# A turned copy ahead of the third group's exponentials, and rotary angles made inside the last feed of the first block

## The chip, the cores and the metric

One core of one Trainium2 chip runs the whole program. The metric is the device time in microseconds. The kernel before was timed three times: 2276.24 us is the median (2274.07 to 2278.8). All times below are microseconds from the start of the span of one profiled execution.

## The reference

Two model blocks run one after the other on 256 tokens of width 1024, in float32, each with two layers.

- The first block's layer is a mixer, a layer norm, a feed and a layer norm. The mixer makes 10 projections of `x`; two attention groups A and B of 4 heads (A with rotary turns on q and k, B with a forgetting bias), a spatial gating branch and a pooling branch; the four results are joined and multiplied by `w_o`. The feed is `h = x @ w_up`, a causal convolution of width 3 along the tokens, `silu(gate) * val`, then `@ w_down` (inner width 2816).
- The second block's layer is an RMS norm, a mixer with a delta-rule branch, a sparse attention branch and a memory branch, and a gated feed.
- The second block's sparse attention turns its q, k and index vectors by angles that depend on the input `positions`:

```python
ang = positions.astype(jnp.float32)[..., None] * inv_freq
cos = jnp.cos(ang)[:, :, None, :]
```

So the tables of sines and cosines of the second block depend on `positions` alone, and not on `x`.

## The kernel before

**One stream of weights.** All large products go through one object, `Stream` (`main`). The weights are cut into chunks of 1 MB, called sources; a source is two halves of 128x1024. For each half, SyncE (SP) loads the raw weights into one of 3 slots (L328), ScalarE (ACT) makes a rounded copy `w_hi` (`high`, L339), GpSimd (POOL) makes the rest `w_lo = w_raw - w_hi` (`low`, L348), and TensorE (PE) does three products per tile (L147, L148, L149). There are 4 slots for `w_hi` and `w_lo`, so `high` of half h waits for the product of half h-4. The load of source n waits until `low` of the last half of source n-3 is done. A unit is one named piece of the stream with its output bank and with what ACT and VectorE (DVE) do at its end.

**Order by hand.** Each engine runs its own program in order. A stage calls `main.act(act, pos)`, `main.dve(dve, pos)` or `main.pe(pe, pos)`, which issues all of the stream's work up to that half, and then adds its own instructions. For ACT, position q issues `high` of half q+3 first, then what the units that end there want. For DVE there is only what units want at their ends. SP runs the `sp` functions of the stages in the order of the stages, and `send(sp, upto)` issues the loads of the stream up to a source, each after its wait.

**The first block's mixer** (`Mixer1`) has four score groups: 0 and 1 are branch A's first and second 128 queries, 2 and 3 are branch B's. A group goes through `scores` (PE), `weigh` (DVE: mask, maximum, L728 to L731), `exponentials` (ACT, L631), `normalise` (DVE: reciprocal L738, product with it L739), `turn` (PE transposes, L524), `turned_copy` (ACT copies the transposes to SBUF, L639), `weighted` (PE, L534), `weighted_high` (ACT, L649) and a low part (DVE, L819). `weigh(2)` and `weigh(3)` wait for `turn(0)` and `turn(1)`, since they write over the same score tiles. PE's `turn(1)` waits for `turned_copy(0)`, for `weigh(2)`'s mask and for `normalise(1)`. PE's `weighted(0)` waits for `weigh(3)`'s mask, and `turn(2)` behind it for `normalise(2)`. PE's `weighted(1)` waits for `turned_copy(2)`.

**The first block's feed** (`Feed1`) has 33 units of two halves each: unit 0 up0, 1 val0, 2 up1, 3 val1, 4 down0, 5 up2, 6 val2, 7 down1, 8 up3, 9 val3, 10 down2, 11 up4 and so on. At the end of an up or val unit ACT makes the first tap and DVE the other two (L876). After a val unit DVE makes `hid` (L888). After up2 DVE also makes the low part of `hid` of pair 1 (`hid_lo`, L898), which the products of down1 wait for (`hid_low`); in general the low part of pair i-1 is made at the end of up i.

**SP in the last feed of the first block.** The stage ahead of the feed is `Norm1` with the key `ln1`. Its `sp` function is `send` up to 12 sources past the last source of the mixer, that is up to unit 11 of the feed. In layer 0 a DMA of `ln_rows` follows it (L1058). `Norm1` with the key `ln2` then sends the rest of the feed.

**The start of the second block.** The last `Norm1` ends the first block, `Norm2` normalises for the second (its low parts, `x_lo`, L1146), and `Mixer2` begins. Its first unit is `sm` (two halves). Its halves 0 to 3 have their `w_hi` and `w_lo` before the norm. ACT issues `high` of halves 4 and 5, reads `small` and `ik` from the bank of `sm` (L1347, L1348), makes exponentials and logarithms in turns with DVE (L2079 to L2099), and only then issues `high` of half 6. In front of all this DVE has `angles` (L2180 to L2191) and ACT has two Sin activations (L1899, L1900), for the tables of the sparse attention. The positions are loaded by SP at the same place (L1535).

Of the kernel before, what the change touches and what calls it, by code (L numbers as in the profile page):

```python
# [23 lines left out]
I32 = mybir.dt.int32  # L24
ALU = mybir.AluOpType
ACT = mybir.ActivationFunctionType
AX_X = mybir.AxisListType.X

P = 128
T = 256  # L30
# [3 lines left out]
DEPTH = 2  # L34
# [98 lines left out]
class Chain:  # L133
# [5 lines left out]
    def step(self, ins):  # L139
        self.n += 1  # L140
        ins.then_inc(self.sem, 1)
        self.eng.wait_ge(self.sem, self.n)
# [278 lines left out]
class Mixer1:  # L421
# [199 lines left out]
    def act(self, act):  # L621
# [3 lines left out]
        def exponentials(g):  # L625
            name, qt, qk, y0, v0 = self.groups[g]
            nk = (qt + 1) * P
            act.wait_ge(*sig.at("shifted", l, g))
            for h in range(4):
                v = m["sm"][g][:, h, 0:nk]  # L630
                ins = act.activation(v, v, ACT.Exp, bias=m["mx"][:, g, h:h + 1], scale=0.125,  # L631
                                     accum_out=m["sum"][:, g, h:h + 1])
            ins.then_inc(*sig.up("exped", l, g))
# [45 lines left out]
        exponentials(1)  # L679
        main.act(act, self.at(17))  # L680
        exponentials(2)
        main.act(act, self.at(18))
        turned_copy(0)
        main.act(act, self.at(19))
# [24 lines left out]
    def dve(self, dve):  # L709
# [100 lines left out]
        weigh(2)  # L810
        normalise(1)
        weigh(3)
        normalise(2)
        normalise(3)
# [9 lines left out]
class Feed1:  # L824
# [107 lines left out]
    def pe(self, pe):  # L932
        self.net.main.pe(pe, self.end())

    def act(self, act):
        self.net.main.act(act, self.end())

    def dve(self, dve):
        self.net.main.dve(dve, self.end())

# [380 lines left out]
class Mixer2:  # L1321
# [209 lines left out]
    def sp(self, sp):  # L1531
        net, l, sig, m = self.net, self.l, self.net.sig, self.net.mem2
        if l == 0:
            sp.wait_ge(*sig.at("x_final", 3))
            sp.dma_start(m["turns"][:, 0, :].bitcast(I32), net.a["positions"].to_broadcast([P, T])  # L1535
                         ).then_inc(*sig.up("pos_loaded", by=16))
        net.main.send(sp, net.main.halves[self.u["sm"].first + 76][0])
        sp.wait_ge(*sig.at("scored2", l, 3))
        sp.dma_start(m["mem"], net.a["mem"].rearrange("(t p) d -> p t d", p=P)).then_inc(*sig.up("mem_loaded", l, by=16))
# [345 lines left out]
    def act(self, act):  # L1885
# [10 lines left out]

        if l == 0:
            act.wait_ge(*sig.at("reduced"))
            act.activation(net.tables[:, 2:4, :], m["angle"][:, :, :], ACT.Sin).then_inc(*sig.up("sined", 0))  # L1899
            act.activation(m["half_sine"][:, :, :], m["angle"][:, :, :], ACT.Sin, scale=0.5).then_inc(*sig.up("sined", 1))  # L1900
        main.act(act, self.at(2))
# [167 lines left out]
    def dve(self, dve):  # L2069
        net, l, sig = self.net, self.l, self.net.sig  # L2070
        K, main, m, bank = net.K, net.main, net.mem2, net.bank
        step, prm = net.dve_chain.step, net.prm2
        if l == 0:
            self.angles(dve)
        dve.tensor_scalar(m["half_bias"][:, :], prm(l, "b_gate"), 0.5, None, ALU.mult).then_inc(*sig.up("half_bias", l))
# [93 lines left out]
        main.dve(dve, 2 * (self.units[-1].last + 1))  # L2169

    def angles(self, dve):
        net, sig, m = self.net, self.net.sig, self.net.mem2
        K, step = net.K, net.dve_chain.step
        magic = 1.5 * 2.0 ** 23
        c1 = 6.28125
        c2 = float((np.float32(2 * np.pi - c1).view(np.int32) // 4096 * 4096).astype(np.int32).view(np.float32))
        c3 = 2 * np.pi - c1 - c2
        pos, a, k, h = m["pos"][:, :], m["angle"][:, :, :], m["turns"][:, :, :], m["half_sine"][:, :, :]
        dve.wait_ge(*sig.at("pos_loaded"))
        step(dve.tensor_copy(pos, m["turns"][:, 0, :].bitcast(I32)))  # L2180
        for j in range(2):
            ins = dve.tensor_scalar(a[:, j, :], pos, K("freq")[:, j:j + 1], None, ALU.mult)
        step(ins)
        step(dve.tensor_scalar(k, a, 1.0 / (2 * np.pi), magic, ALU.mult, ALU.add))
        step(dve.tensor_scalar(k, k, magic, None, ALU.subtract))
        for c in (c1, c2, c3):
            step(dve.scalar_tensor_tensor(a, k, -c, a, ALU.mult, ALU.add))
        dve.tensor_scalar(a, a, 3.1415925, -3.1415925, ALU.min, ALU.max).then_inc(*sig.up("reduced"))
        dve.wait_ge(*sig.at("sined", 1))
        step(dve.tensor_tensor(h, h, h, ALU.mult))  # L2190
        step(dve.tensor_scalar(net.tables[:, 0:2, :], h, -2.0, 1.0, ALU.mult, ALU.add))  # L2191

# [197 lines left out]
class Net:  # L2390
# [88 lines left out]
    def second_memory(self, area):  # L2479
# [11 lines left out]
        m["set"] = [[place(f"{n}_set{hf}", 16 * hf + 4 * i, [P, 4, T])[:, :, :] for i, n in enumerate("qkvz")] for hf in range(2)]  # L2491
        m["pos"], m["turns"] = place("pos", 16, [P, T]), place("turns", 17, [P, 2, T])
        m["angle"], m["half_sine"] = place("angle", 19, [P, 2, T]), place("half_sine", 21, [P, 2, T])
        m["half"] = h = {}
# [78 lines left out]
    def run(self):  # L2573
        nc, sig, a, main, const = self.nc, self.sig, self.a, self.main, self.const
        xT = self.xn[:, :, :].rearrange("p t (k c) -> p (t k) c", c=T)
        with nc.Block() as block:
            @block.sync
            def _(sp):
# [16 lines left out]
                for s in self.stages:  # L2595
                    if isinstance(s, (Norm1, Norm2, Mixer2, Final)):
                        s.sp(sp)
# [105 lines left out]
```

## Time and profile before

| what | us |
|---|---|
| median of 3 runs | 2276.24 |
| the profiled execution's own time | 2277.58 |
| its span | 2275.8 |
| PE busy | 2163.2 (95%) |
| POOL busy | 1498.6 (66%) |
| ACT busy | 1073.0 (47%) |
| DVE busy | 955.9 (42%) |
| mean granted TensorE clock | 0.972 of full |

PE is busy for 95% of the span, so time is won or lost where PE stands still, or where its clock is granted at half. Busy time of the other engines matters only where PE, at that moment, waits for them. The matmuls' ends in the records are modelled: a matmul with 256 columns is shown as 0.28 us and one starts every 0.12 us at full clock.

### The profile page before, as it was taken

What the parts mean: (1) busy time and instruction counts of PE and PEld (TensorE: products, weight loads), DVE (VectorE), ACT (ScalarE), POOL (GpSimd) and SP (SyncE); (2) the same over time, 40 slices, a digit from 0 to 9 for tenths busy, and PEclk for the clock granted to TensorE, in tenths of its full rate; (3) what the DMA queues carried; (4) which work ended last, traced back from release to release, by engine and by line L of the source; (5) the groups of instructions that cost most, each with busy time, mean ns of one, the idle gap of its engine ahead of it and who ended that gap; (6) DMA issues with size and microseconds to landing.
All of it is one profiled execution on the core that took longest, in us unless ns stands there. A gap on an engine that the chain in (4) does not pass through costs nothing.

```text
span 2275.8 us, 35984 instructions
## 1 busy us (share of the span) xinstructions
PE 2163.2 (95%) x15336; PEld 2001.3 (88%) x15336; DVE 955.9 (42%) x1484; ACT 1073.0 (47%) x1517; POOL 1498.6 (66%) x632
## 2 busy tenths in 40 slices
PE   8989989899969899999999899998999999999998
PEld 7789978799959888989999899898889899998998
DVE  4353256442375537477112211456374681123112
ACT  4555555555545352255444444473441454544444
POOL 6679877698846234356778688663243566786886
PEclk9999999999989999999999999999999999999999
DMA  8345544355524113134445455442131344454553
GB/s 338 132 146 204 185 139 161 117 180 187 184 84 147 60 71 106 64 128 167 151 164 185 148 185 185 156 145 90 56 112 56 130 148 149 157 182 150 184 185 133
DMA packets 47183, 333.05 MB, mean 146 GB/s; under 512 B 5168, under 2 KB 5552, under 8 KB 7856
## 3 DMA queue, kind: packets, MB, share of 16 engines
q1 hardware_dynamic: 47024, 330.76, 41.9%
q8 instruction: 121, 1.98, 0.4%
q14 instruction: 38, 0.31, 0.0%
HBM read 329.69 MB, written 1.05 MB: 145 GB/s over the span
## 4 chain that ended last, share of the span: by engine, by line
PE 62%; DVE 8%; issue 1%; ACT 1%; POOL 0%; DVEq 0%; ACTq 0%
PE bank L147 14%; PE bank L149 14%; PE bank L148 14%; PE y L147 2%; PE y L149 2%; PE y L148 2%; PE bank L1749 2%; PE bank L1748 1%; PE bank L1739 1%; DVE conv L1384 1%; PE bank L1672 1%; PE bank L1794 1%; PE bank L1791 1%; PE bank L1774 1%; DVE sq L1583 1%
## 5 line engine op out<-in xcount | busy, mean ns | idle before, releaser
L348 POOL TENSOR_TENSOR w_lo<-w_raw,w_hi 128x1024 fp32r<-128x1024 f32 x602 | 1463.0, 2437 | 759.7 <-ACT w_hi L339 759.6
L339 ACT ACTIVATE w_hi<-w_raw 128x1024 fp32r<-128x1024 f32 x602 | 635.7, 1059 | 1009.4 <-PE bank L149 838.9
L147 PE MATMUL bank<-x_hi,w_hi 128*128 128x256 f32 x2960 | 876.6, 296 | 21.6 <-POOL w_lo L348 17.1
L148 PE MATMUL bank<-x_lo,w_hi 128*128 128x256 f32 x2960 | 848.4, 287 | 0.0
L149 PE MATMUL bank<-x_hi,w_lo 128*128 128x256 f32 x2960 | 848.3, 287 | 0.0
L147 PEld LDWEIGHTS bank<-x_hi,w_hi 128*128 128x128 f32 x2960 | 579.1, 196 | 44.9 <-issue 24.4
L148 PEld LDWEIGHTS bank<-x_lo,w_hi 128*128 128x128 f32 x2960 | 579.0, 196 | 10.5 <-issue 8.6
L149 PEld LDWEIGHTS bank<-x_hi,w_lo 128*128 128x128 f32 x2960 | 578.4, 195 | 0.0
L876 DVE SCALAR_TENSOR_TENSOR conv<-bank,par_sb,conv 128x254 f32<-128x254 f32 (+1 forms) x176 | 76.8, 478 | 240.1 <-ACT conv L864 238.6
L1246 DVE TENSOR_TENSOR hid_lo<-hid,hid_hi 128x512 fp32r<-128x512 f32 x22 | 45.1, 2048 | 241.2 <-ACT hid_hi L1241 241.2
L147 PE MATMUL y<-w_hi,hid_hi 128*128 128x512 f32 x352 | 139.9, 397 | 3.3 <-DVE hid_lo L898 3.3
L149 PE MATMUL y<-w_hi,hid_lo 128*128 128x512 f32 x352 | 138.9, 395 | 0.0
L148 PE MATMUL y<-w_lo,hid_hi 128*128 128x512 f32 x352 | 138.9, 395 | 0.0
L1384 DVE SCALAR_TENSOR_TENSOR conv<-bank,par_sb,conv 128x255 f32<-128x255 f32 (+1 forms) x144 | 62.6, 477 | 63.8 <-ACT conv L1375 62.1
L147 PEld LDWEIGHTS y<-w_hi,hid_hi 128*128 128x128 f32 x352 | 66.3, 188 | 19.2 <-DVE hid_lo L898 5.4
L149 PEld LDWEIGHTS y<-w_hi,hid_lo 128*128 128x128 f32 x352 | 66.2, 188 | 15.7
L148 PEld LDWEIGHTS y<-w_lo,hid_hi 128*128 128x128 f32 x352 | 66.2, 188 | 13.8
L1491 DVE SCALAR_TENSOR_TENSOR gate<-gate,bank 128x512 f32<-128x512 f32 x16 | 11.0, 688 | 130.5 <-PE bank L149 130.5
L1749 PE MATMUL bank<-ti,es 128*128 128x128 f32 x320 | 61.0, 290 | 4.1 <-DVE es L2275 4.1
L1748 PE MATMUL bank<-es,ti 128*128 128x128 f32 x256 | 51.8, 286 | 7.0 <-DVE es L2275 7.0
L1749 PEld LDWEIGHTS bank<-ti,es 128*128 128x128 f32 x320 | 49.6, 205 | 4.5 <-DVE es L2275 4.5
L2347 DVE SCALAR_TENSOR_TENSOR sc<-index,tokq,sc 128x128 f32<-128x128 f32 (+1 forms) x28 | 52.6, 1878 | 1.0
(397 smaller groups left out, 3243.6 us busy)
## 6 DMA issues: line engine op xcount, KB each, us to landing
w_raw<-w SPq DMA_DIRECT2D x300, 1024.0 KB, 4.8
ln_rows<-ln_rows SPq DMA_DIRECT2D x4, 1024.0 KB, 7.2
mem_tok<-mem SPq DMA_DIRECT2D x2, 1024.0 KB, 4.9
const_sb<-const SPq DMA_DIRECT2D x1, 1536.0 KB, 9.3
par_sb<-par SPq DMA_DIRECT2D x2, 553.5 KB, 10.7
xn<-xT SPq DMA_DIRECT2D x1, 1024.0 KB, 4.9
w_raw<-w SPq DMA_DIRECT2D x2, 512.0 KB, 5.4
x_tok<-x SPq DMA_DIRECT2D x1, 1024.0 KB, 7.2
```

What stands on the lines that cost most here:

```text
L147: pe.matmul(out, lhs[0], rhs[0], start=start, stop=False, skip_group_check=skip)
L148: pe.matmul(out, lhs[0], rhs[1], start=False, stop=False, skip_group_check=skip)
L149: return pe.matmul(out, lhs[1], rhs[0], start=False, stop=stop, skip_group_check=skip)
L339: act.activation(self.hi[:, h % HALVES, :], self.raw[:, n % RAWS, i * HW:(i + 1) * HW], ACT.Copy).then_inc(*sig.up("high", h))
L348: pool.tensor_tensor(self.lo[:, h % HALVES, :], self.raw[:, n % RAWS, i * HW:(i + 1) * HW], self.hi[:, h % HALVES, :].bitcast(F32), ALU.su ...
L876: ins = dve.scalar_tensor_tensor(cb[:, j, tap:T], view[:, j, 0:T - tap], taps[:, 2 - tap, c0 + j:c0 + j + 1], cb[:, j, tap:T], ALU.mult, A ...
L1246: dve.tensor_tensor(net.hs2[1][:, 2 * (i % 3):2 * (i % 3) + 2, :], m["hid"][:, i % 2, :, :], net.hs2[0][:, 2 * (i % 3):2 * (i % 3) + 2, :] ...
L1384: ins = dve.scalar_tensor_tensor(cb[:, j, tap:T], two(b)[:, j, 0:T - tap], taps[:, 3 - tap, c0 + j:c0 + j + 1], cb[:, j, tap:T], ALU.mult, ...
L1583: net.dve_chain.step(dve.tensor_tensor(raw, raw, cos.unsqueeze(1).to_broadcast([P, w, T]), ALU.mult))
L1748: pe.matmul(yd[g][:, c], h["ti"][:, n, :], h["y"][:, n, :], start=True, stop=True)
L1749: mm = pe.matmul(cp[g][:, c], h["y"][:, n, :], h["ti"][:, n, :], start=True, stop=True)
L2347: ins = dve.scalar_tensor_tensor(sc, m["r"][qt][:, (h % 2) * 4 + h // 2, :], m["tokq"][:, qt, 4, h:h + 1], mask if h == 0 else sc, ALU.mul ...
```

## The change

Three edits. First, in the mixer of the first block (both layers), ACT makes `turned_copy(0)` before `exponentials(2)`, and DVE makes `normalise(2)` before `weigh(3)`. Second, the angles of the second block are made in the feed of layer 1 of the first block: DVE's operations stand in pairs behind the units 4, 7, 10, 13, 19 and 22, ACT's two Sin activations behind unit 16. Third, the load of the positions moves to a new `sp` function of `Feed1`, and `Feed1` is added to the stages whose `sp` is called; the four tiles of the angles lie at other addresses, over constants that only the first block's mixer reads.

```diff
@@ Mixer1.act
         main.act(act, self.at(17))
+        turned_copy(0)
+        main.act(act, self.at(18))
         exponentials(2)
-        main.act(act, self.at(18))
-        turned_copy(0)
         main.act(act, self.at(19))
@@ Mixer1.dve
         normalise(1)
+        normalise(2)
         weigh(3)
-        normalise(2)
         normalise(3)
@@ Feed1
+    def after_unit(self, n):
+        return 2 * (self.units[n].last + 1)
+
+    def sp(self, sp):
+        net, sig, m = self.net, self.net.sig, self.net.mem2
+        if self.l == DEPTH - 1:
+            sp.wait_ge(*sig.at("var", "ln1", self.l, 1))
+            sp.dma_start(m["turns"][:, 0, :].bitcast(I32), net.a["positions"].to_broadcast([P, T])
+                         ).then_inc(*sig.up("pos_loaded", by=16))
@@ Feed1.act
+            main.act(act, self.after_unit(16))
+            act.wait_ge(*sig.at("reduced"))
+            act.activation(net.tables[:, 2:4, :], m["angle"][:, :, :], ACT.Sin).then_inc(*sig.up("sined", 0))
+            act.activation(m["half_sine"][:, :, :], m["angle"][:, :, :], ACT.Sin, scale=0.5).then_inc(*sig.up("sined", 1))
@@ Feed1.dve
+            main.dve(dve, self.after_unit(4))
+            dve.wait_ge(*sig.at("pos_loaded"))
+            step(dve.tensor_copy(pos, m["turns"][:, 0, :].bitcast(I32)))
+            for j in range(2):
+                ins = dve.tensor_scalar(a[:, j, :], pos, net.K("freq")[:, j:j + 1], None, ALU.mult)
+            step(ins)
+            main.dve(dve, self.after_unit(7))
+            step(dve.tensor_scalar(k, a, 1.0 / (2 * np.pi), magic, ALU.mult, ALU.add))
+            step(dve.tensor_scalar(k, k, magic, None, ALU.subtract))
+            main.dve(dve, self.after_unit(10))
+            for c in (c1, c2):
+                step(dve.scalar_tensor_tensor(a, k, -c, a, ALU.mult, ALU.add))
+            main.dve(dve, self.after_unit(13))
+            step(dve.scalar_tensor_tensor(a, k, -c3, a, ALU.mult, ALU.add))
+            dve.tensor_scalar(a, a, 3.1415925, -3.1415925, ALU.min, ALU.max).then_inc(*sig.up("reduced"))
+            main.dve(dve, self.after_unit(19))
+            dve.wait_ge(*sig.at("sined", 1))
+            step(dve.tensor_tensor(h, h, h, ALU.mult))
+            main.dve(dve, self.after_unit(22))
+            step(dve.tensor_scalar(net.tables[:, 0:2, :], h, -2.0, 1.0, ALU.mult, ALU.add))
@@ Mixer2.sp, Mixer2.act, Mixer2.dve: the same operations are taken out
-        if l == 0:
-            sp.wait_ge(*sig.at("x_final", 3))
-            sp.dma_start(m["turns"][:, 0, :].bitcast(I32), ...)
...
-        if l == 0:
-            act.wait_ge(*sig.at("reduced"))
...
-        if l == 0:
-            self.angles(dve)
@@ Net.run
-                    if isinstance(s, (Norm1, Norm2, Mixer2, Final)):
+                    if isinstance(s, (Norm1, Feed1, Norm2, Mixer2, Final)):
                         s.sp(sp)
```

## Rows read from the trace of the kernel before

**Rows 1.** The page's chain that ended last: shares of the span by engine.

```profile
PE 62%; DVE 8%; issue 1%; ACT 1%; POOL 0%; DVEq 0%; ACTq 0%
```

**Rows 2.** Waits of PE: us in total, times, longest.

```profile
PE t L524 <- ACT pt L639: 4.3, 2, 2.1
```

**Rows 3.** Timeline, start of block two: start, us, engine, line, [idle before <-releaser].

```profile
652.35 1.28 ACT L1899 ACT_TABLE_LOAD   x1
653.32 0.28 DVE L2180 CAST pos<-turns 128x256 f32<-128x256 int32 x1
660.03 4.78 POOL L348 TENSOR_TENSOR w_lo<-w_raw,w_hi 128x1024 fp32r<-128x1024 f32 x2 [25.41 <-ACT w_hi L339]
660.22 2.27 DVE L2075 TENSOR_SCALAR half_bias<-par_sb 128x24 f32<-128x24 f32 x1
660.81 1.13 ACT L1347 ACTIVATE small<-bank 8x256 f32<-8x256 f32 x3
662.68 2.29 DVE L2079 TENSOR_SCALAR y<-small,par_sb 8x256 f32<-8x256 f32 x1
665.79 0.59 PE L1598 MATMUL bank<-ik,const_sb 128*128 128x256 f32 x2
670.53 1.99 ACT L339 ACTIVATE w_hi<-w_raw 128x1024 fp32r<-128x1024 f32 x2
671.65 14.30 POOL L348 TENSOR_TENSOR w_lo<-w_raw,w_hi 128x1024 fp32r<-128x1024 f32 x6 [6.83 <-ACT w_hi L339]
674.05 0.45 PE L147 MATMUL bank<-x_hi,w_hi 128*128 128x256 f32 x1 [4.79 <-POOL w_lo L348]
677.69 0.28 PE L149 MATMUL bank<-x_hi,w_lo 128*128 128x256 f32 x1
```

**Rows 4.** Windows: PE, PEld, DVE, ACT, POOL busy (x), PEclk, DMA share, GB/s.

```profile
82.50:85.00 2.50, 0.35 (x4) 0.30 (x4) 0.37 (x1) 2.50 (x7) 0.75 (x1) 1.00 0.71 295
```

**Rows 5.** Timeline of SP: weight loads and the DMA behind one.

```profile
174.61 0.33 SPq L328 DMA_DIRECT2D w_raw<-w  x1
174.98 0.43 SPq L1058 DMA_DIRECT2D ln_rows<-ln_rows  x1
...
488.90 0.33 SPq L328 DMA_DIRECT2D w_raw<-w  x1
```

**Rows 6.** DMA issues: KB each, us from issue to landing.

```profile
w_raw<-w SPq DMA_DIRECT2D x300, 1024.0 KB, 4.8
turns<-positions SPq DMA_DIRECT2D x1, 128.0 KB, 2.9
```

**Rows 7.** Timeline of the last feed of block one, units 5 to 8.

```profile
477.24 1.78 DVE L876 SCALAR_TENSOR_TENSOR conv<-bank,par_sb,conv 128x255 f32<-128x255 f32 x4 [8.58 <-ACT conv L864]
478.94 2.25 DVE L898 TENSOR_TENSOR hid_lo<-hid,hid_hi 128x512 fp32r<-128x512 f32 x1
481.24 0.50 PE L147 MATMUL y<-w_hi,hid_hi 128*128 128x512 f32 x1 [0.35 <-DVE hid_lo L898]
483.65 17.49 POOL L348 TENSOR_TENSOR w_lo<-w_raw,w_hi 128x1024 fp32r<-128x1024 f32 x7
```

**Rows 8.** Timeline of the first block's mixer, layer 0.

```profile
57.85 2.69 DVE L748 TENSOR_TENSOR aqk<-aqk,const_sb 128x512 f32<-128x512 f32 x1
79.92 0.69 DVE L728 TENSOR_TENSOR sm<-s,forget 128x512 f32<-128x512 f32 x1 [10.31 <-PE t L524]
81.65 1.23 DVE L739 TENSOR_TENSOR sm<-sm,rc 128x1024 f32<-128x1024 f32 x1
84.08 0.57 ACT L639 ACTIVATE pt<-t 128x512 f32<-128x512 f32 x1
84.70 1.09 PE L524 MATMUL t<-const_sb,sm 128*128 128x128 f32 x8 [2.15 <-ACT pt L639]
89.87 0.66 PE L524 MATMUL t<-const_sb,sm 128*128 128x128 f32 x4 [0.71 <-DVE sm L739]
93.23 1.14 PE L534 MATMUL o<-pt,abv 128*64 128x128 f32 x16
```

More of the change, by code:

```diff
@@ L933, in pe @@
         self.net.main.pe(pe, self.end())
-    def act(self, act):
-        self.net.main.act(act, self.end())
-    def dve(self, dve):
-        self.net.main.dve(dve, self.end())
+    def after_unit(self, n):
[6 more added lines that the diff above has]
+                         ).then_inc(*sig.up("pos_loaded", by=16))
@@ new lines, in act @@
+    def act(self, act):
+        net, sig, m, main = self.net, self.net.sig, self.net.mem2, self.net.main
+        if self.l == DEPTH - 1:
+            main.act(act, self.after_unit(16))
+            act.wait_ge(*sig.at("reduced"))
+            act.activation(net.tables[:, 2:4, :], m["angle"][:, :, :], ACT.Sin).then_inc(*sig.up("sined", 0))
+            act.activation(m["half_sine"][:, :, :], m["angle"][:, :, :], ACT.Sin, scale=0.5).then_inc(*sig.up("sined", 1))
+        main.act(act, self.end())
@@ new lines, in dve @@
+    def dve(self, dve):
+        net, sig, m, main = self.net, self.net.sig, self.net.mem2, self.net.main
+        if self.l == DEPTH - 1:
+            step = net.dve_chain.step
+            magic = 1.5 * 2.0 ** 23
+            c1 = 6.28125
+            c2 = float((np.float32(2 * np.pi - c1).view(np.int32) // 4096 * 4096).astype(np.int32).view(np.float32))
+            c3 = 2 * np.pi - c1 - c2
+            pos, a, k, h = m["pos"][:, :], m["angle"][:, :, :], m["turns"][:, :, :], m["half_sine"][:, :, :]
+            main.dve(dve, self.after_unit(4))
[18 more added lines that the diff above has]
+            step(dve.tensor_scalar(net.tables[:, 0:2, :], h, -2.0, 1.0, ALU.mult, ALU.add))
+        main.dve(dve, self.end())
@@ L1532, in sp @@
         net, l, sig, m = self.net, self.l, self.net.sig, self.net.mem2
-        if l == 0:
-            sp.wait_ge(*sig.at("x_final", 3))
-            sp.dma_start(m["turns"][:, 0, :].bitcast(I32), net.a["positions"].to_broadcast([P, T])
-                         ).then_inc(*sig.up("pos_loaded", by=16))
         net.main.send(sp, net.main.halves[self.u["sm"].first + 76][0])
@@ L1895, in key_log @@
                            ).then_inc(*sig.up("key_inverse", l, hf, j))
-        if l == 0:
-            act.wait_ge(*sig.at("reduced"))
-            act.activation(net.tables[:, 2:4, :], m["angle"][:, :, :], ACT.Sin).then_inc(*sig.up("sined", 0))
-            act.activation(m["half_sine"][:, :, :], m["angle"][:, :, :], ACT.Sin, scale=0.5).then_inc(*sig.up("sined", 1))
         main.act(act, self.at(2))
@@ L2169, in dve @@
         main.dve(dve, 2 * (self.units[-1].last + 1))
[L2171 to L2191, printed above, removed]
     def prepare_dve(self, dve, hf, unit_key):
@@ L2491, in second_memory @@
         m["set"] = [[place(f"{n}_set{hf}", 16 * hf + 4 * i, [P, 4, T])[:, :, :] for i, n in enumerate("qkvz")] for hf in range(2)]
-        m["pos"], m["turns"] = place("pos", 16, [P, T]), place("turns", 17, [P, 2, T])
-        m["angle"], m["half_sine"] = place("angle", 19, [P, 2, T]), place("half_sine", 21, [P, 2, T])
+        m["pos"], m["turns"] = place("pos", 0, [P, T]), place("turns", 1, [P, 2, T])
+        m["angle"], m["half_sine"] = place("angle", 3, [P, 2, T]), place("half_sine", 5, [P, 2, T])
         m["half"] = h = {}
```

## The prediction

> **What bounds the kernel now.** I read the page first, its chain of waits: 62% of the span by TensorE (PE) and 8% by VectorE (DVE) [rows 1]. PE is the bound, so I look only for places where PE stands still or runs at half clock, and ask what each part of the change does there. Then I read PE's waits and the timelines of three places. At the start of block two PE stands still for 4.79 us until the low part of half 6 is made [rows 3]. In each mixer of block one it waits 2.15 us ahead of `turn(1)` for `turned_copy(0)` (4.3 us over two layers, [rows 2]) and 0.71 us ahead of `turn(2)` for `normalise(2)` [rows 8]. In the last feed of block one it hardly waits: 0.35 us ahead of down1 [rows 7]. So the change has about 4.8 + 2 x 2.9 us of stalls to win, and the feed is where something can be lost.
>
> **Part 1, the angles leave the start of block two.** DVE's angles begin at 653.32, and `half_bias`, which follows them, at 660.22 [rows 3]. Without them `half_bias` can start at 653.4. The next step, `y`, then waits for ScalarE's (ACT) copies of `small` and `ik`. These need the product of half 1. Half 4's product ends at 665.79 [rows 3] and a half is 24 matmuls at 0.12 us = 2.88 us, so half 1 ends at 657.15. ACT makes `high` of half 5 first (1.0 us), then the copies (1.13 + 0.39), and ends at 659.9. Meanwhile GpSimd (POOL) makes the low part of half 5, from about 658.5 to 660.9. `half_bias` took 2.27 us for 24 columns: it began 0.19 us after a POOL operation and ended when that ended (660.03 + 2.39); `y`, at 662.68, ended with the second [rows 3]. So I let `y` end with POOL again, at 661.05 instead of 664.97: 3.9 us earlier. The chain behind it (exponential, logarithm, scans, to `high` of half 6 at 670.53) has nothing that moves otherwise, so half 6's low part comes at 670.15 and PE, which has ended half 5 at 669.2, stands still for 0.9 us instead of 4.79.
>
> After the stall of 4.79 us the clock was half: the 17 matmuls from 674.05 to 677.69 took 3.64 us instead of 2.04, a loss of 1.6 us [rows 3]. A stall of 2.15 us left the clock full (1.00 in that window, [rows 4]), so a stall of 0.9 us will too. Part 1 gives 3.9 + 1.6 = **-5.5 us**. Its ends are -6.4 (no stall is left) and -3.5 (0.4 us later, clock still half).
>
> **Part 2, the wait for the positions in the feed.** DVE waits for `pos_loaded` behind unit 4, in front of unit 5 (up2). SP, though, comes to `Feed1.sp` only after `Norm1.sp`, which sends the stream up to unit 11. The load of unit 11 waits for the low part of unit 8's last half. Layer 0 shows the same place in SP's order: `ln_rows` was issued at 174.98, 0.37 us behind a weight load at 174.61; in layer 1 the corresponding weight load is at 488.90 [rows 5]. POOL's run from 483.65 has two halves (2.5 us each) ahead of it, 16 and 17, the halves of unit 8 [rows 7]. So the positions are asked for at 489.3. With DVE standing still, POOL isn't held up by it (about 1 us in its last operations), so I put the issue at 488.3.
>
> Who waits? Behind the waiting DVE instruction stands all of up2's work: its taps (477.24 before) and `hid_lo` of pair 1 (478.94 before), and down1's first matmul, at 481.24, waits for that [rows 7]. There is no deadlock: the low part of half 17 needs only the product of half 13 (val2), which needs nothing of DVE behind unit 4. But PE stops in front of down1.
>
> Landing: alone the positions took 2.9 us, a weight load 4.8 [rows 6]. Bounds: 488.3 + 2.9 = 491.2; behind the whole weight load, 487.9 + 4.8 = 492.7 and some 1.7 us for its own small packets, 494.4. I take 493.5, near the upper end, since the weight load is asked for only 0.4 us ahead. Then DVE: the copy and the first two products, 1.0 us (three short operations like the 0.28 us copy); taps to `hid_lo` 478.94 - 477.24 = 1.70; `hid_lo` 0.7 instead of 2.25, as POOL is idle. PE starts down1 at 493.5 + 3.45 = 496.95, against 481.24: **+15.7 us**. Restart at half clock: +1.6, as in part 1. POOL's backlog is worked off in the stall, so the next waits for `hid_lo` (0.35 to 0.4 us each) may go: -0.4. Sum of part 2: **+16.9 us**, between +14.6 (lands at 491.2) and +19.5.
>
> The other feed pieces I cost at nothing. DVE was idle for 8.58 us ahead of up2's taps [rows 7], behind the down unit, and up3, up4 and so on have the same gap; two operations of 0.7 us, each held up by POOL by at most 2.4, need 6.2. ACT's Sin pair behind unit 16 costs two table loads (1.28 us each [rows 3]) and two activations under 1.0 us, at most 4.6 us, in a stream that is four halves (11.5 us) ahead of PE. Were that cover gone, each would cost its own length once.
>
> **Part 3, the mixer's two swaps.** ACT can start `turned_copy(0)` when DVE starts `weigh(2)` on the same release, 79.92 [rows 8]. Before, it came behind the exponentials, at 84.08. By that alone PE would start `turn(1)` when `normalise(1)` ends, 82.9 instead of 84.70: -1.8, and with the 0.71 us -2.5 a layer. But ACT now goes on to `high` of half 21 at 80.39 and POOL starts its low part 1.12 us later (670.53 to 671.65 is this distance, [rows 3]), at 81.52. `normalise(1)`'s product, two SBUF inputs, comes at 81.65 [rows 8], 0.13 us behind. A product of that kind, L748, started at 57.85 in a POOL operation and took 2.69 us instead of 0.69 [rows 8]. So here it ends at 83.91 + 1.1 = 85.0 and `turn(1)` starts at 85.05, not earlier than before. Then `normalise(2)` (85.25) falls behind the low part of half 22 (85.0 to 87.4) and ends at 87.95; `weigh(3)`, now behind it, has its mask at 89.2 and its maximum at 90.65; `exponentials(3)` ends at 92.65, `high` of half 23 and one small copy follow, and `turned_copy(2)` ends at 94.45. PE reaches `weighted(1)` at 93.23 as before [rows 8] and waits till 94.5. That is **+1.25 us a layer, +2.5 in all**. From the other side, if the product gets in first, POOL waits for it and `normalise(2)` waits for POOL: `turned_copy(2)` at 92.4, -0.85 a layer; with no collision at all -2.5 a layer. Ends: -4.9 and +3.5; I take +2.5, since 0.13 us decides and stands on POOL's side in both layers, which have equal spacings.
>
> The trace agrees with the Trainium skill's page "SBUF — State Buffer", section "Who interferes with whom": DVE with two SBUF inputs and a GpSimd operation that reads SBUF exclude one another, and the one that issues first holds the port for its whole instruction. By a rule that shared bandwidth instead, `normalise(1)` would end near 83.3 and this part would gain, not lose; 57.85 to 60.54 speaks against it.
>
> **Sum.** -5.5 + 16.9 + 2.5 = +13.9 us. On the profiled execution's own time, 2277.58 (span 2275.8), that is 2291.5; it lies 1.3 above the median of the runs, 2276.24, from which it is 2290.1. I say 2291.
>
> **The rivals.**
> - A. *The stall is there, the mixer swaps win.* For it: PE's waits of 2.15 and 0.71 us are real, and 0.13 us is a thin margin. -5.5 + 16.9 - 1.7 = +9.7, 2287; with no collision +6.5, 2284. Chance 0.2.
> - B. *The positions land before DVE asks* (this one ends on the other side). It needs SP to issue them before the low part of half 13 or so, that is, to be at `Feed1.sp` by the time unit 4 ends (about 469). Then DVE's idle 8.58 us hides the three short operations, part 2 is zero, and -5.5 +2.5 gives 2274 (-5.5 - 4.9 gives 2267). It decides at a landing by about 476, before up2's taps; each us later costs one. Against it: SP's order and the 174.98 of layer 0. Chance 0.08.
> - C. *The gain of part 1 does not come*: something else holds half 6, as ACT's chain now waits for POOL's second low part at each small DVE operation. Each adds up to 2.4 us; +13.9 + 5.5 = 2297. For it: `half_bias` and `y` were both held up. Against it: POOL is idle from 660.9 on until half 6. Chance 0.1.
>
> **How the numbers follow.** Main case 0.62, 2291 (its own range 2288 to 2295, from the bounds of the landing). A, B and C as above. The range 2283 to 2297 holds the main case, all of A and C. A measurement of this kernel can tell 0.2%, 4.6 us, from no change. Slower by more: the main case, A (its no-collision end is +6.5) and C: 0.91. Within 0.2%: part of B, 0.04. Faster: the rest of B, 0.05.
>
> **What would show it.** In the profile after: the load of positions by SP directly behind the weight load near 488; DVE idle from 468.7 until about 493; one PE stall of some 15 us ahead of down1, released by `hid_lo` (L898), the largest of the whole profile outside the norms, with half clock behind it. At the start of block two: a stall under 1.5 us with clock 1.00. In the mixer: the product of L739 in group 1 near 3.3 us long instead of 1.23, and PE waiting ahead of `weighted(1)` for ACT's `pt`. The forecast is wrong if the positions are issued much before 488, or if PE passes down1 on time.

## The result and the profile after

The changed kernel takes 2290.26 us (median of 4 runs, 2289.86 to 2292.14) against 2276.09 us for the kernel before in runs beside it: a ratio of 1.0063, interval 1.0046 to 1.0081. That is 14.2 us slower. The prediction was 2291 us. The profiled execution after took 2289.86 us with a span of 2288.1, 12.3 us more than the span before. The profiled execution before was 1.5 us above the median of its kernel and this one 0.4 us below, which is the 1.9 us between the two differences.

First the waits of PE, in us, times and longest, of the kernel after.

```profile
PE y L147 <- DVE hid_lo L898: 18.1, 7, 15.5
PE bank L147 <- POOL w_lo L348: 13.4, 3, 11.4
PE t L524 <- DVE sm L739: 5.0, 2, 2.5
...
PE o L534 <- ACT pt L639: 1.2, 1, 1.2
```

The same list of the kernel before:

```profile
PE bank L147 <- POOL w_lo L348: 17.1, 3, 11.4
...
PE y L147 <- DVE hid_lo L898: 3.3, 8, 0.5
```

The wait for `hid_lo` grew by 14.8 us, by one stall of 15.5 us. The wait for POOL's low part fell by 3.7 us. In the mixer the wait for `turned_copy` of 4.3 us [rows 2] is gone, and 5.0 us for DVE's `sm` (1.4 us before) stand in its place, with 1.2 us ahead of `weighted(1)`.

**The feed.** Timelines after: start, us, engine, line, [idle before <-releaser]. The first two rows are SP's, the next two POOL's, then DVE's, and PE's first matmul of down1.

```profile
489.80 0.33 SPq L328 DMA_DIRECT2D w_raw<-w  x1
490.18 0.43 SPq L942 DMA_DIRECT2D turns<-positions  x1
...
485.14 4.64 POOL L348 TENSOR_TENSOR w_lo<-w_raw,w_hi 128x1024 fp32r<-128x1024 f32 x2
504.25 2.39 POOL L348 TENSOR_TENSOR w_lo<-w_raw,w_hi 128x1024 fp32r<-128x1024 f32 x1 [14.47 <-ACT w_hi L339]
...
469.07 1.58 DVE L888 TENSOR_TENSOR hid<-gates,conv 128x512 f32<-128x512 f32 x1
494.92 0.29 DVE L965 CAST pos<-turns 128x256 f32<-128x256 int32 x1 [24.27 <-DMA turns<-positions]
495.25 0.62 DVE L967 TENSOR_SCALAR angle<-pos,const_sb 128x256 f32<-128x256 f32 x2
495.90 1.78 DVE L876 SCALAR_TENSOR_TENSOR conv<-bank,par_sb,conv 128x255 f32<-128x255 f32 x4
497.60 0.68 DVE L898 TENSOR_TENSOR hid_lo<-hid,hid_hi 128x512 fp32r<-128x512 f32 x1
...
498.33 0.80 PE L147 MATMUL y<-w_hi,hid_hi 128*128 128x512 f32 x1 [15.45 <-DVE hid_lo L898]
```

Read it from the bottom: PE waits 15.45 us for `hid_lo`, which is made as soon as the taps are; the taps stand behind the two products and the copy; and these wait for the positions, which SP asked for directly behind a weight load. That load was free to go when POOL ended the second of its two halves (485.14 + 4.64). DVE stood idle for 24.27 us.

Windows after, columns as in [rows 4]: behind that stall, and at the start of block two.

```profile
498.30:502.30 4.00, 3.97 (x10) 3.15 (x11) 3.09 (x7) 0.10 (x1) 0.00 (x0) 0.55 0.00 0
688.30:692.30 4.00, 3.97 (x33) 3.98 (x34) 3.89 (x10) 3.94 (x7) 4.00 (x2) 1.00 0.16 27
```

PE did 10 matmuls in 4 us at a granted clock of 0.55 (0.5 is half) after 15.45 us idle. At the start of block two the clock is full. Its timeline after:

```profile
671.43 0.17 DVE L2109 TENSOR_SCALAR half_bias<-par_sb 128x24 f32<-128x24 f32 x1
678.05 1.15 DVE L2113 TENSOR_SCALAR y<-small,par_sb 8x256 f32<-8x256 f32 x1 [6.20 <-ACT ik L1392]
688.33 0.38 PE L147 MATMUL bank<-x_hi,w_hi 128*128 128x256 f32 x1 [0.96 <-POOL w_lo L348]
```

`half_bias`, which took 2.27 us in [rows 3], takes 0.17, and the stall of 4.79 us is one of 0.96.

**Where the time went.** Both programs have the same 15336 matmuls in the same order, so the stretch between two matmuls of the same number can be subtracted. The mixer stretches hold `turn(1)` and `weighted(1)` (81.5 to 93.7 and 394.1 to 413.3 us in the profile before), the feed's is 480.3 to 500.4 and that of block two 651.5 to 680.0. In us:

```
stretch                                      before   after   difference
mixer of block one, layer 0                    12.2    13.3     +1.1
mixer of block one, layer 1                    19.2    20.1     +0.9
last feed, with down1                          20.2    36.3    +16.1
start of block two                             28.4    23.1     -5.3
the rest                                     2189.3  2188.8     -0.5
start of the span to the last matmul         2269.3  2281.6    +12.3
```

The rest hides stretches of block two that moved by -2.4 to +1.7 us each, though the change touches nothing in them.

**The mixer of layer 0**, timeline after:

```profile
80.82 2.37 POOL L348 TENSOR_TENSOR w_lo<-w_raw,w_hi 128x1024 fp32r<-128x1024 f32 x1 [1.19 <-ACT w_hi L339]
81.00 3.27 DVE L739 TENSOR_TENSOR sm<-sm,rc 128x1024 f32<-128x1024 f32 x1
84.39 2.65 DVE L739 TENSOR_TENSOR sm<-sm,rc 128x512 f32<-128x512 f32 x1
84.41 1.06 PE L524 MATMUL t<-const_sb,sm 128*128 128x128 f32 x8 [2.51 <-DVE sm L739]
```

POOL starts 0.18 us ahead of the product of `normalise(1)`, which takes 3.27 us where it took 1.23 [rows 8], and PE stands still for 2.51 us. From there the two layers differ. Windows after, layer 0 (first two) and the same place in layer 1:

```profile
84.40:86.40 2.00, 1.99 (x11) 1.77 (x12) 2.00 (x1) 0.96 (x2) 2.00 (x1) 0.77 0.00 0
86.40:88.40 2.00, 2.00 (x6) 1.57 (x5) 1.97 (x3) 0.14 (x1) 0.09 (x1) 0.50 0.45 111
...
401.00:405.00 4.00, 3.97 (x26) 3.13 (x27) 3.96 (x3) 1.02 (x1) 1.92 (x1) 1.00 0.27 61
```

and PE at `weighted(1)`, in layer 0 and in layer 1:

```profile
93.70 1.15 PE L534 MATMUL o<-pt,abv 128*64 128x128 f32 x16
...
409.92 1.15 PE L534 MATMUL o<-pt,abv 128*64 128x128 f32 x16 [1.20 <-ACT pt L639]
```

In layer 1 the clock stays full and PE waits 1.20 us for `turned_copy(2)`. In layer 0 the clock falls to half, which costs PE about as much, and it arrives late enough to find the copy ready. Why the clock fell in one layer and not in the other isn't shown.

### The profile page after: what moved, and what is told of

Read it like the earlier page. It is cut to its first block, busy times and chain, and to the rows that moved or that the text cites. A ratio compares the mean times of both kernels' runs of the same rounds, so it can differ in the third digit from the quotient of the medians.

```text
span 2288.1 us, 35988 instructions
## 1 busy us (share of the span) xinstructions
PE 2162.6 (95%) x15336; PEld 2000.1 (87%) x15336; DVE 971.5 (42%) x1484; ACT 1071.9 (47%) x1516; POOL 1503.0 (66%) x632
## 4 chain that ended last, share of the span: by engine, by line
PE 60%; DVE 9%; ACT 1%; issue 1%; POOL 0%; DVEq 0%; ACTq 0%
PE bank L147 13%; PE bank L148 13%; PE bank L149 13%; PE y L147 2%; PE y L149 2%; PE y L148 2%; PE bank L1789 2%; PE bank L1788 1%; DVE sc L2359 1%; PE bank L1779 1%; DVE conv L1428 1%; PE bank L1712 1%; PE bank L1831 1%; PE bank L1834 1%; PE bank L1814 1%
## 5 line engine op out<-in xcount | busy, mean ns | idle before, releaser
L147 PE MATMUL bank<-x_hi,w_hi 128*128 128x256 f32 x2960 | 875.4, 296 | 17.7 <-POOL w_lo L348 13.4
L148 PEld LDWEIGHTS y<-w_lo,hid_hi 128*128 128x128 f32 x352 | 66.6, 189 | 13.9
## 6 DMA issues: line engine op xcount, KB each, us to landing
par_sb<-par SPq DMA_DIRECT2D x2, 553.5 KB, 10.7
```

Source lines behind the costliest of these rows:

```text
L147: pe.matmul(out, lhs[0], rhs[0], start=start, stop=False, skip_group_check=skip)
L148: pe.matmul(out, lhs[0], rhs[1], start=False, stop=False, skip_group_check=skip)
```

## The experiments

Line numbers shift a little from kernel to kernel; the names don't. The kernel before ran beside each set: 2277.58 us (29 runs) in the first, 2277.97 (20) in the second, 2276.95 (17) in the third.

### The positions asked for early

```
 Feed1.sp:  return                        # no load here
 Norm1.sp, layer 1, key ln1:
+  net.main.send(sp, net.main.halves[self.after().last][0] + 1 + 5)
+  sp.wait_ge(*sig.at("var", "ln1", l, 1))
+  sp.dma_start(turns <- positions) ... up("pos_loaded", by=16)
   net.main.send(sp, ... + 12)            # as before
```

> The changed kernel with one edit: SP issues the load of the positions after the load of the feed's unit 4, not after that of unit 11. Theory (the positions come late because of SP's order): the stall of 15.45 us ahead of down1 and the 1.6 us of half clock behind it go; DVE's wait for the positions ends at once. Time 2290.3 - 16.9 = 2273.4 us, 0.12% under the kernel before. Rival (the DVE operations of the angles themselves, which share SBUF with GpSimd's operations, cost the time in the feed): the load's place changes little, the time stays above 2285, and PE still waits for hid_lo by several us. Rival (the mixer's swaps carry most of the loss): above 2285 too.

Measured: 2273.57 us, ratio to the kernel before 0.9987 (0.9973 to 1.0001). The down1 stretch is 20.7 us, against 36.3 after and 20.2 before; the start of block two 24.9. The 12 runs lie in two groups, seven from 2272.65 to 2273.72 and five from 2277.43 to 2278.64, so that the median falls on the forecast of 2273.4 says less than it seems. Timeline, and a window at the start of block two, columns as in [rows 4]:

```profile
468.29 1.38 DVE L962 CAST pos<-turns 128x256 f32<-128x256 int32 x1
469.70 3.75 DVE L964 TENSOR_SCALAR angle<-pos,const_sb 128x256 f32<-128x256 f32 x2
...
481.06 0.50 PE L147 MATMUL y<-w_hi,hid_hi 128*128 128x512 f32 x1 [0.46 <-DVE hid_lo L898]
...
652.00:656.00 4.00, 4.00 (x20) 4.00 (x20) 1.97 (x7) 0.55 (x2) 0.00 (x0) 0.50 0.00 0
```

The three operations are there, held up by POOL (0.91 us after, 5.1 us here), and lie in DVE's idle time; PE waits 0.46 us. So the operations in the feed cost at most 0.5 us, and the place of the load in SP's order about 16. At the start of block two the stall is again 0.96 us, but the half clock that follows the norm lasts 4 us into this stretch (the last row), where in the kernel after it had ended (1.00 from 669.70 to 673.70): that is the 1.8 us between 24.9 and 23.1. The same kernel, profiled once more:

> early_positions, unchanged, profiled once more, with the same theory and rival: the stretch at the start of block two again 23 to 25 us, the mixers 13.1 and 20.1 us; differences of 2 us or more in the delta-rule stretches or at the rotary products of the second mixer.

It took 2274.93 us, with the same 20.7 and 24.9 us in these two stretches; that the late positions cost the time is shown. The differences of 2 us that I expected further on didn't come: from the feed to the end the two profiles agree within 0.1 us (212.4 us in the first delta-rule stretch in both), and the 2.3 us between them arise ahead of 330 us. Whether this kernel beats the one before isn't: the interval reaches 1.

### The positions in between

The same with `+ 1 + 10` for `+ 1 + 5`.

> The changed kernel with the load of the positions behind the weight load of the feed's unit 9, not of unit 11 (4.9 us ahead of early enough, 12 us before the changed kernel's place). Theory (the stall is the landing time plus DVE's chain of 3.4 us, less PE's own arrival at down1): load asked for at about 478.4, lands at 483.1, hid_lo ends at 486.5, or at 488.1 if GpSimd's low part of half 16 is in front of it; PE's stall ahead of down1 is 3.1 to 5 us, where it was 15.45. Time 2273.6 + 3 to + 6.5 = 2276.6 to 2280 us, with the half clock behind the stall at the upper end. Rival (something of the wait doesn't go with the landing time): a stall above 8 us or none.

Measured: 2288.98 us, ratio 1.0047 (1.0032 to 1.0062); the down1 stretch is 28.7 us, +8.5 on before. Timeline, SP's row first:

```profile
476.18 0.43 SPq L1099 DMA_DIRECT2D turns<-positions  x1
...
481.16 0.74 DVE L962 CAST pos<-turns 128x256 f32<-128x256 int32 x1 [12.62 <-DMA turns<-positions]
481.93 3.65 DVE L964 TENSOR_SCALAR angle<-pos,const_sb 128x256 f32<-128x256 f32 x2
...
483.04 4.74 POOL L348 TENSOR_TENSOR w_lo<-w_raw,w_hi 128x1024 fp32r<-128x1024 f32 x2
...
487.31 1.02 DVE L898 TENSOR_TENSOR hid_lo<-hid,hid_hi 128x512 fp32r<-128x512 f32 x1
488.39 0.79 PE L147 MATMUL y<-w_hi,hid_hi 128*128 128x512 f32 x1 [7.62 <-DVE hid_lo L898]
```

The positions landed about when they were meant to (5.0 us after the issue), and the stall is 7.62 us, not the 3.1 to 5 us of the theory and just under the rival's 8. It is larger than the landing alone makes it, because POOL was at work when DVE woke: the copy and the two products took 4.4 us where the kernel after, with POOL idle, needed 0.95. So the stall follows the landing, and here the work of POOL put 3.5 us on top. The time missed its forecast of 2276.6 to 2280 by far more: against the early positions this stretch gives only 8.0 of the 15.4 us between the medians. In the profiles another 5.9 us stand in the first delta-rule stretch of block two (218.3 us against 212.4), which the edit doesn't touch.

### The swaps, taken out and put in alone

`swaps_undone` is the kernel after with the order of before in the mixer; `swaps_alone` is the kernel before with both swaps.

```
 ACT:  exponentials(1); act(at(17));
-      turned_copy(0); act(at(18)); exponentials(2)
+      exponentials(2); act(at(18)); turned_copy(0)
 DVE:  normalise(1);
-      normalise(2); weigh(3)
+      weigh(3); normalise(2)
```

> The changed kernel with the mixer's two swaps undone (turned_copy(0) behind exponentials(2) and normalise(2) behind weigh(3), as before); the late positions stay. Theory (the swaps cost 1.1 to 1.3 us a layer by the collision of normalise(1) with GpSimd's low part): 2290.3 - 2.5 = 2287.8 us, and normalise(1)'s product is 1.23 us long again. Rival (the swaps win, as PE's waits of 2.15 and 0.71 us a layer suggest, and something else is worse than I take it): 2290.3 + 1.7 to + 4.9, 2292 to 2295. Rival (the swaps are the main loss): 2276.

Measured: 2296.17 us (6 runs, 2290.65 to 2297.68), ratio 1.0072 (1.0048 to 1.0096). The mixer of layer 0 is 12.2 us again, as the theory says, but that of layer 1 is 20.0 us, hardly less than the 20.1 of the kernel after, since the clock fell to half in it (0.56 from 402 to 405). The stall ahead of down1 is 15.4 us. The total missed the theory's 2287.8 us; it lies above even the 2292 to 2295 of the rival by which the swaps win, though its interval overlaps that of the kernel after. The profile is 6.2 us longer than that of the kernel after. What is longer lies in stretches that the edit doesn't touch (3.6 us ahead of layer 1's mixer, 2.7 in the first delta-rule stretch, 1.7 at the start of block two, 1.1 in the feed), and others are shorter. The first is a stall that the kernel after doesn't have, in layer 1 ahead of its scores:

```profile
PE s L513 <- DVE aqk L749: 3.0, 1, 3.0
```

> The kernel before with the mixer's two swaps alone. Theory: 2276.1 + 2.5 = 2278.6 us; PE waits 2.5 us ahead of turn(1) for normalise(1) in both layers, and its clock may fall to half behind a wait of that length. Rival (the swaps take away the waits of 2.15 and 0.71 us): 2276.1 - 4.9 = 2271.2 us.

Measured: 2281.45 us, ratio 1.0014 (0.9998 to 1.0029); the mixers are 13.2 and 20.3 us, +1.0 and +1.1, as the theory says; the interval of the total takes in no change. Layer 0's timeline:

```profile
84.04 1.06 PE L524 MATMUL t<-const_sb,sm 128*128 128x128 f32 x8 [2.50 <-DVE sm L739]
...
93.14 1.15 PE L534 MATMUL o<-pt,abv 128*64 128x128 f32 x16 [1.20 <-ACT pt L639]
```

Here the clock stayed full (1.00 from 84.40 to 88.40) behind the same stall as in the kernel after, and PE waits 1.20 us at `weighted(1)`: the path of the prediction, in layer 0 as well.

### Each swap alone

One run each, on the kernel before, so that only the stretches can be compared and not the totals.

> The kernel before with turned_copy(0) ahead of exponentials(2) in ACT's order alone. Theory (the collision lies here): normalise(1)'s product takes 3.27 us and PE waits 2.5 us ahead of turn(1), 0.35 us longer than before; by the clock after such a wait 0 to 1.5 us more. PE comes to weighted(1) 0.4 to 1.8 us later a layer, time 2277 to 2279.7 us. Rival (the copy's order alone wins the 2.15 us): PE at turn(1) near 83.0, time 2272.

Measured: 2277.32 us; mixers 12.1 and 19.1, -0.1 each.

```profile
81.85 3.27 DVE L739 TENSOR_TENSOR sm<-sm,rc 128x1024 f32<-128x1024 f32 x1
85.26 1.06 PE L524 MATMUL t<-const_sb,sm 128*128 128x128 f32 x8 [2.51 <-DVE sm L739]
89.98 0.66 PE L524 MATMUL t<-const_sb,sm 128*128 128x128 f32 x4 [0.28 <-DVE sm L739]
```

The collision with POOL is there, and yet PE loses nothing further on; I had expected a loss of 0.4 to 1.8 us a layer.

> The kernel before with normalise(2) ahead of weigh(3) in DVE's order alone. Theory: normalise(2) fits in between 83.2 and 84.1, ahead of GpSimd's next low part, so turn(2) no longer waits 0.71 us; weighted(1) then waits for turned_copy(2) by some 0.3 us. PE gains 0.4 to 0.7 us a layer; time 2275.3 us. Rival (this swap carries the loss): PE comes to weighted(1) at 94.0 or later, where it was 93.23.

Measured: 2278.74 us; mixers 11.9 and 18.8, -0.3 and -0.4.

```profile
93.49 1.15 PE L534 MATMUL o<-pt,abv 128*64 128x128 f32 x16 [0.36 <-ACT pt L639]
```

So neither swap alone loses. The +1 us a layer needs both: the copy's swap puts POOL ahead of `normalise(1)`, and the other then puts `weigh(3)` behind a held-up `normalise(2)`, which makes `turned_copy(2)` late.

### The high part made later

To take the collision away without taking the swap away, ACT's high part of half 21 goes behind the exponentials, on top of the early positions.

```
-      turned_copy(0); act(at(18)); exponentials(2)
+      turned_copy(0); exponentials(2); act(at(18))
```

> early_positions with one more edit: in the mixer ACT makes turned_copy(0), then exponentials(2), and only then goes on in the stream (high of half 21). So GpSimd's low part of half 21 starts at about 84.2 us and not 81.5, and normalise(1) and normalise(2) are over before it. Theory (the swaps fail only by that collision): normalise(1)'s product takes 1.23 us, PE's turn(1) starts 1.8 us earlier than in the kernel before and turn(2) doesn't wait, -2.5 us a layer against the kernel before; with part 1's -5.5 us the time is 2276.1 - 5.5 - 4.9 = 2265.7 us, 0.46% under the kernel before. Rival (the collision isn't the cause, the new order of ACT and DVE is longer in itself): no better than early_positions, 2273.4.

Measured: 2277.46 us, ratio 0.9995 (0.9981 to 1.0009); mixers 11.9 and 18.8 us, -1.2 and -1.3 against the early positions. Layer 0's timeline:

```profile
81.83 1.22 DVE L739 TENSOR_TENSOR sm<-sm,rc 128x1024 f32<-128x1024 f32 x1
86.88 2.31 DVE L731 TENSOR_SCALAR mx<-mx 128x4 f32<-128x4 f32 x1
...
83.20 1.06 PE L524 MATMUL t<-const_sb,sm 128*128 128x128 f32 x8 [0.46 <-DVE sm L739]
...
93.05 1.15 PE L534 MATMUL o<-pt,abv 128*64 128x128 f32 x16 [1.14 <-ACT pt L639]
```

The total, forecast at 2265.7 us, is that of the kernel before and above the rival's 2273.4, and against the kernel before the mixers gain 0.3 and 0.4 us where 2.5 was forecast for each. The first step of the theory holds all the same. With POOL elsewhere the product takes 1.22 us again and PE waits 0.46 us, not 2.5. That shows the collision to be the cause of the stall ahead of `turn(1)`. But another has come: the 4 columns of `mx`, scaled by -0.125, now fall beside POOL and take 2.31 us, and PE waits 1.14 us at `weighted(1)`. The next kernel moves that scaling to ACT:

```
-  dve.tensor_scalar(mx, mx, -0.125, None, ALU.mult)
+  act.activation(mx, mx, ACT.Copy, scale=-0.125)     # ahead of the exponentials
```

> late_high with one more edit: the maximum's scaling by -0.125, a 128x4 operation on DVE (L731) that GpSimd held up for 2.1 us in late_high, is made by ACT. Theory (what is left of the loss in late_high is this one small operation behind GpSimd's low part): exponentials(3) starts near 87.0 and not 89.2, turned_copy(2) is ready ahead of weighted(1), and the mixer's stretch from scores to the second output unit takes 10.8 us a layer (11.9 in late_high, 12.2 before, 13.1 in the changed kernel). Time, fast executions of each: 2 us under early_positions and 4 to 5 us under the kernel before, 2268 to 2273 us. Rival (weighted(1) waits for something else, or ACT's added operations cost as much): 11.5 us or more.

Measured: 2277.41 us (12 runs, 2270.15 to 2282.06), ratio 0.9997 (0.9986 to 1.0009); mixers 10.7 and 17.7.

```profile
92.19 1.15 PE L534 MATMUL o<-pt,abv 128*64 128x128 f32 x16
```

The scaling takes 0.20 us on ACT, the wait at `weighted(1)` is gone, and the mixers are 2.4 us a layer shorter than in the early positions. The total, forecast at 2268 to 2273 us, doesn't show it. The profiles of this kernel and of the one ahead of it both have the stall of 3.0 us ahead of layer 1's scores, which the early positions haven't, and that eats more than one layer's gain; the first delta-rule stretch takes 218.4 us here against 212.4.

### The angles early, without the swaps

> early_positions with the mixer's two swaps undone: the move of the angles alone, with the positions loaded in time. Theory (the move is worth -5.5 us at the start of block two, and nothing else changes): 2276.1 - 5.5 = 2270.6 us; PE waits 0.9 to 1.0 us and not 4.79 ahead of half 6. Rival (the gain at the start of block two is given back later in block two): above 2274. By the swaps' cost of about 1.1 us a layer it is 2.2 us under early_positions.

Measured: 2278.57 us (12 runs, 2267.51 to 2280.79), ratio 0.9995 (0.9981 to 1.0008): not 2270.6, but on the side of the rival. The gain of part 1 is there all the same:

```profile
670.23 0.39 PE L147 MATMUL bank<-x_hi,w_hi 128*128 128x256 f32 x1 [0.96 <-POOL w_lo L348]
```

The start of block two takes 23.1 us (-5.3). In its profile four later stretches of block two give it back: 218.6 us against 216.4, 215.9 against 214.0, 157.4 against 153.9, 185.6 against 184.3, together +8.9. Work and order in them are those of the kernel before.

### The kernel before, once more

> The kernel before, unchanged, profiled once more. Theory (the executions of one kernel differ by up to 5 us in the delta-rule stretch of block two and at the rotary products of the second mixer, by the order in which DVE and GpSimd come to the shared SBUF interface and by when the clock is granted at half): some stretch differs from the first profile by 2 us or more, while the mixers of block one (12.2 us each), the stall-free feed (20.2 us) and the start of block two (28.4 us) stay within 0.5 us. Rival (each kernel has its own fixed times there): all stretches agree within 0.5 us.

It took 2275.7 us; the span is 2273.9, against 2275.8 in the profile shown above. Inside it one stretch of 400 matmuls, around layer 1's rotary work, took 66.3 us and not 62.7. DVE, POOL and PE there, timeline:

```profile
374.04 2.71 DVE L749 TENSOR_TENSOR aqk<-aqk,rope 128x512 f32<-128x512 f32 x1
...
373.58 2.63 POOL L348 TENSOR_TENSOR w_lo<-w_raw,w_hi 128x1024 fp32r<-128x1024 f32 x1 [1.33 <-ACT w_hi L339]
...
376.80 1.52 PE L513 MATMUL s<-aqk 64*128 64x128 f32 x8 [3.03 <-DVE aqk L749]
```

In the first profile of the same kernel the same product took 0.69 us, at 375.22, and PE did not wait:

```profile
375.22 0.69 DVE L749 TENSOR_TENSOR aqk<-aqk,rope 128x512 f32<-128x512 f32 x1
```

One program, two outcomes of who comes first, DVE or POOL, 3.6 us apart. It is also the stall that the profile of `swaps_undone` had and that of the kernel after had not.

That some stretch differs by 2 us or more is what the theory says; the first delta-rule stretch, which it names too, took 216.4 us in both profiles. Layer 0's mixer (12.2 us) and the feed (20.2) stayed as they were. The theory failed in two places that were to stay within 0.5 us: layer 1's mixer took 20.0 us and not 19.2, and the start of block two 26.7 and not 28.4. Clock in the mixer, then the stall at the start of block two:

```profile
401.00:405.00 4.00, 3.49 (x14) 3.01 (x15) 1.81 (x2) 3.28 (x5) 3.94 (x2) 0.63 0.07 31
676.35 0.39 PE L147 MATMUL bank<-x_hi,w_hi 128*128 128x256 f32 x1 [2.96 <-POOL w_lo L348]
```

In the mixer PE came out of the stall of 2.15 us at half clock, where it had stayed full in the first profile. At the start of block two half clock lasted 4 us into the stretch (0.50 from 654 to 658), PE came later to the same wait, stood still for 2.96 us and not 4.79, and the clock stayed full behind it.

## Why the prediction was right

Its order of events held but for one step in part 3, and so did its total: +14.2 us between the medians, forecast +13.9. That the total is met to 0.3 us is in part luck. In the two profiles both losses came out smaller than forecast: the three parts sum to +12.8 us, not +13.9, and the whole to +12.3; the medians lie 1.9 us further apart than the profiles do.

- **Part 1** was forecast at -5.5 and measured -5.3 us in this pair of profiles. The stall of 4.79 us became 0.96 (forecast 0.9) with the clock full; `y` took 1.15 us and no longer 2.29. The same 0.96 us stands in the kernel without the swaps. Rival C, something else holding half 6, didn't come. But the size hangs on the clock that the norm leaves behind, which the forecast doesn't ask about. Over all profiles the stretch takes 26.7 to 28.8 us with the angles in it and 23.1 to 24.9 without. In the old order the wait for the angles hides a slow start of PE (a stall of 2.96 us instead of 4.79); in the new one nothing hides it, and with half clock for the first 4 us in both, `before_again` against the early positions, the gain is 1.8 us.
- **Part 2** was forecast at +16.9 and measured +16.1 us. Of it the stall grew from 0.35 to 15.45 us, +15.1 (forecast 15.7), the half clock made up about 1.6, and shorter waits behind it gave 0.6 back. The positions were asked for behind the weight load, as forecast (490.18; this place is 2.0 us later in the profile after, so 488.2 against 488.3), and landed 4.7 us after their issue. I had put this at 5.2; the 0.5 us is most of the miss. The 1.7 us for small packets in my bound comes from no row, and the upper end of +19.5 doesn't follow from it (a landing at 494.4 gives +17.8); measured are landings of 4.7 to 5.3 us directly behind a weight load. Rival B needed them earlier; the experiment with early positions shows what it would have brought, 2273.6 where the rival said 2274.
- **Part 3** was forecast at +2.5 and measured +2.0 us. POOL did come first, by 0.18 us in layer 0 (forecast 0.13), and the product took 3.27 us (forecast 3.35). The late high part, with POOL elsewhere, gives 1.22 us again. The Trainium skill's page "SBUF — State Buffer", section "Who interferes with whom", states that a DVE instruction with two SBUF inputs contends with a GpSimd instruction that reads SBUF. Both measurements agree with it.
- **The step of part 3 that failed.** In layer 1, and in layer 0 of the swaps alone, the loss is the wait of 1.20 us at `weighted(1)`, as worked out. In layer 0 of the kernel after, and in layer 1 of the swaps alone (a clock of 0.50 from 401 to 403), it is half clock instead, at about the same price. So one sentence of the forecast failed: PE "reaches `weighted(1)` at 93.23 as before" took the clock for full, from a stall of 2.15 us that had left it so. It doesn't always: of the ten such stalls in five profiles with the copy in its old place (before twice, swaps undone, the other swap alone, angles early without swaps) two were followed by half clock, both in layer 1, and of the twelve stalls of 2.5 us in six profiles also two. So the half clock is not shown to be a cost of the swaps. At full clock the mixers take 12.2 and 19.2 us without them and 13.1 or 13.2 and 20.1 with them, +0.9 or +1.0 each; at half clock layer 1 takes 20.0 and 20.3, +0.3. The +2.5 was worked out from the wait at `weighted(1)`, and only one layer of the kernel after has that wait; that the other lost as much is luck.
- **Costs put at nothing.** The pieces in the feed were indeed hidden: 0.5 us at most with the positions early. ACT's two table loads were over-costed: in the profile after, the two Sin activations (0.61 and 0.62 us, at 558.16 and 558.68) have no table load beside them.

**What stays open.** The stretches of block two behind the change differ between kernels by more than the small edits bring: the first delta-rule stretch took 212.4 us with the positions early, 216.4 before and 219.6 with the swaps undone. In the profiles such stretches make up most of what `swaps_undone` is slower than the kernel after, and most of what the gains of 1 to 5 us in a stage lack in the total. The granted clock there goes with it in part (0.96 in the first, 0.94 before). I think it is the same contest of DVE and POOL, moved by a shift of start times, and the stalls that follow; no run isolates it. Against mere chance from execution to execution speaks that two profiles of the early positions agree within 0.1 us from the feed on, and two of the kernel before in the first delta-rule stretch (216.4); yet the second profile of the kernel before differs by 3.6 us in layer 1. None of the versions tried is shown to be faster than the kernel before.

## What to carry to other kernels

A load that is moved in the program of a queue that works in order must be timed from its new place in that queue, by what the instruction ahead of it waits for: here SP stood behind weight loads until 490 us while its user asked for the data at 471. Then ask which engine waits for it, what is queued behind that wait, and what PE needs of it. When a kernel's runs differ by some us by themselves, compare stretches between the same matmuls, and don't sum small stage gains into a total before a timed run shows them. Before a stage's gain is taken for fixed, ask what the removed wait had been hiding: here it hid a slow start of PE.

## What the runs showed of the hardware

- A tiny operation can pay the whole length of a POOL operation beside it: `tensor_scalar` of 128x4 took 2.31 us, of 128x24 2.27, each instead of 0.17.
- Products with two SBUF inputs of 128x512 that POOL held up ended 0.54 to 0.56 us after POOL's operation (374.04 + 2.71 against 373.58 + 2.63), those of 1024 columns 1.1 us after it (81.00 + 3.27 against 80.82 + 2.37).
- Who comes first can change from one execution to the next of the same program (62.7 or 66.3 us in one stretch).
- The 128 KB of positions landed in 2.9 us alone, and in 4.7, 5.0 and 5.3 us (kernel after, positions in between, positions early) where SP asked for them directly behind a weight load.
- Six profiles (after, swaps alone, the copy's swap alone, positions early twice, positions in between) have the same stall of 2.5 us ahead of `turn(1)` in both layers: in ten of the twelve places the clock stayed full, in two it fell to 0.50. Five profiles have a stall of 2.15 us there: in eight of the ten places the clock stayed full, in two it fell to half (0.63 and 0.67 from 401 to 405).
- Behind a stall of 4.79 us the clock was half in the kernel before (674 to 678); in `swaps_alone` it fell 1.4 us after the end of a stall of 3.29 us; behind one of 2.96 us in `before_again` and of 0.96 us in the kernel after it was full (1.00).
